# A mixture-of-experts kernel: the first expert's tokens gathered as high and low parts, and fewer zero products ahead of the router's last tile

## The reference

```
def moe_swiglu(h, w_router, w_gu, w_down):        # 8 experts, top 2
    t = h.reshape(-1, D)
    top_val, top_idx = lax.top_k(t @ w_router, TOP_K)
    top_w = jax.nn.softmax(top_val, axis=-1)
    gates = sum(one_hot(top_idx) * top_w)
    for e in range(N_EXPERTS):                     # silu(t@g) * (t@u) @ w_down[e], width 3584
        out = out + gates[:, e:e + 1] * swiglu(t, w_gu[e], w_down[e])
```

## Time and profile before

| | us |
|---|---|
| median of 3 runs | 1406.62 (1405.25 to 1407.14) |
| the profiled execution's own time | 1406.65 |
| its span in the trace | 1404.8 |
| TensorE busy | 1342.0 |
| VectorE busy | 1172.6 |
| ScalarE busy | 898.4 |

### The profile page before, as it was taken

The page is one execution under the profiler, slowest core; times in us unless marked ns, Lnnn a source line. Parts: engine busy times, 40 slices in busy tenths (PEclk is TensorE's granted clock), DMA queues, the critical chain, the costliest instruction groups (busy, mean ns, idle before and its releaser), DMA issues.

```text
span 1404.8 us, 19513 instructions
## 1 busy us (share of the span) xinstructions
PE 1342.0 (96%) x6901; PEld 1130.2 (80%) x6901; DVE 1172.6 (83%) x950; ACT 898.4 (64%) x745; POOL 76.4 (5%) x93
## 2 busy tenths in 40 slices
PE   5589999999999999999999999999999999999995
PEld 3489999789777888888888888888888888888883
DVE  5866777778869988889888888888888888888883
ACT  3143443464837777777777777777777777777771
POOL 2510000000120000000000000000000000000000
PEclk9779999999999999999999999999999999999998
DMA  9998888759168999999999999999999999999970
GB/s 363 383 326 276 313 309 313 282 196 385 46 233 293 410 393 360 383 383 390 359 392 388 357 395 373 383 367 385 387 350 400 383 362 387 373 391 360 411 285 32
DMA packets 210154, 476.18 MB, mean 339 GB/s; under 512 B 14928, under 2 KB 38560, under 8 KB 210096
## 3 DMA queue, kind: packets, MB, share of 16 engines
q1 hardware_dynamic: 205216, 459.07, 87.6%
q0 software_dynamic: 4880, 16.34, 3.8%
HBM read 466.43 MB, written 8.93 MB: 338 GB/s over the span
## 4 chain that ended last, share of the span: by engine, by line
PE 89%; DVE 7%; ACT 2%; issue 1%; DMA 1%; SPq 0%; DVEq 0%; POOL 0%; POOLq 0%; ACTq 0%
PE ps L1525 28%; PE ps L1527 27%; PE ps L1526 27%; PE ps L1918 2%; DVE rows L1099 1%; DVE rows L1094 1%; DVE wlo L1017 1%; PE ps L1543 1%; DMA raw<-w_mod 1%; DVE rows L1029 1%; DVE rows L1031 1%; PE ps L1750 0%; DVE wlo L1310 0%; PE ps L1884 0%; ACT whi L679 0%
## 5 line engine op out<-in xcount | busy, mean ns | idle before, releaser
L1310 DVE TENSOR_TENSOR wlx<-raw,whx 128x2048 fp32r<-128x2048 f32 x168 | 384.8, 2292 | 97.6 <-ACT whx L909 96.7
L1310 DVE TENSOR_TENSOR wlo<-raw,whi 128x2048 fp32r<-128x2048 f32 x168 | 384.2, 2288 | 4.4 <-ACT whi L909 3.0
L909 ACT ACTIVATE whi<-raw 128x2048 fp32r<-128x2048 f32 x168 | 322.2, 1919 | 88.6 <-PE ps L1527 87.4
L909 ACT ACTIVATE whx<-raw 128x2048 fp32r<-128x2048 f32 x168 | 322.2, 1919 | 82.9 <-PE ps L1527 82.9
L1525 PE MATMUL ps<-whi,thi 128*128 128x512 f32 x508 | 204.5, 402 | 1.0 <-DVE tlo L1282 0.6
L1527 PE MATMUL ps<-whi,tlo 128*128 128x512 f32 x508 | 198.5, 391 | 0.0
L1526 PE MATMUL ps<-wlo,thi 128*128 128x512 f32 x508 | 198.2, 390 | 0.0
L1525 PE MATMUL ps<-whx,thi 128*128 128x512 f32 x452 | 176.8, 391 | 0.5 <-DVE tlo L1282 0.5
L1527 PE MATMUL ps<-whx,tlo 128*128 128x512 f32 x452 | 176.1, 390 | 0.0
L1526 PE MATMUL ps<-wlx,thi 128*128 128x512 f32 x444 | 172.8, 389 | 0.0
L1525 PE MATMUL ps<-thi,whi 128*128 128x256 f32 x480 | 137.5, 286 | 3.1 <-DVE tlo L1021 3.1
(11 more groups left out here) (258 smaller groups left out, 1922.1 us busy)
## 6 DMA issues: line engine op xcount, KB each, us to landing
raw<-moe_w_gu SPq DMA_DIRECT2D x448, 512.0 KB, 6.1
raw<-moe_w_down SPq DMA_DIRECT2D x224, 512.0 KB, 6.3
raw<-w_mod SPq DMA_DIRECT2D x96, 512.0 KB, 5.3
raw<-ffn_w_gu SPq DMA_DIRECT2D x44, 512.0 KB, 5.1
raw<-w_qkv SPq DMA_DIRECT2D x24, 512.0 KB, 5.6
raw<-ffn_w_down SPq DMA_DIRECT2D x22, 512.0 KB, 4.4
raw<-w_o SPq DMA_DIRECT2D x8, 512.0 KB, 5.6
gain<-norm_g POOLq DMA_DIRECT2D x4, 512.0 KB, 4.9
```

The lines of the kernel that those rows point to most:

```text
L909: act.activation(m_hi[m % MRING], raw[:, r % RAW, :], ACT.Copy).then_inc(hi_ready, 1)
L1310: dve.tensor_tensor(m_lo[m % MRING], raw[:, r % RAW, :], m_hi[m % MRING].bitcast(F32), ALU.subtract).then_inc(unit_done, 1)
```

## The change

The gather of expert 0 is done on parts. The high and low parts of the token tiles are made as rows ahead of it: ScalarE writes `h_hi` (`token_high`, 128 x 1024 for each tile), VectorE `h_lo` (`token_low`). `sel_r` is the selection as fp32r. TensorE multiplies each part with `sel_r` by itself, high parts into banks 2 and 3, low parts into banks 4 and 1, so that `thi` and `tlo` are plain copies of the banks. ScalarE copies bank 3 of the router's second tile instead of VectorE. The 24 zero products become 8. In VectorE's stream the two copies of the low banks come ahead of the low part of unit 1, and `select(0)`, which the slot plan still needs in fp32, behind it.

More of the change, by code:

```diff
@@ L242, in build_trunk @@
         sb("scr_mid", [P, 2 * D])
-        sb("scr_end", [P, UNIT])
+        scr_end = sb("scr_end", [P, UNIT], F32R)
         wlx1 = sb("wlx1", [P, UNIT], F32R)
         wlx2 = sb("wlx2", [P, UNIT], F32R)
+        h_hi = scr_end[:, :].rearrange("p (t d) -> p t d", t=T)
+        h_lo = whx1[:, :].rearrange("p (t d) -> p t d", t=T)
+        sel_r = ahi[:, 0:T * P].rearrange("p (t s) -> p t s", t=T)
         o_hi = [whx1[:, :]] + [whi[:, (Q_WO + i) % SPL, :] for i in range(SPL)]
@@ L376, in build_trunk @@
         wo_ps = sem("wo_ps")
-        ht32_rest = sem("ht32_rest")
+        parts_hi = sem("parts_hi")
+        parts_lo = sem("parts_lo")
+        selr_ready = sem("selr_ready")
+        gl_ps = sem("gl_ps")
         counting_ready = sem("counting_ready")
@@ L1325, in _ @@
             expert_low(0, 0)
-            dve.wait_ge(ht_ps, 4 * 2 + 4)
-            dve.tensor_copy(ht32[:, 4:8, P:S], bank(3).rearrange("p (k s) -> p k s", k=4)).then_inc(ht32_rest, 1)
+            def token_low(t):
[3 more added lines that the diff above has]
+            token_low(0)
             dve.wait_ge(lg_ps, 1)
@@ L1837, in router @@
                     if k % 4 == 0:
[L1838 to L1841, removed]
+                        pe.wait_ge(ht32_ready, 2 * t + k // 4 + 1)
                     mm = pe.matmul(ps[:, 4, t * NE:t * NE + NE], ht32[:, k, t * P:t * P + P], wr[:, k, :],
@@ L1868, in experts @@
                 r0, j0, n0 = R_MOE + ps_no * NE * EXPERT_UNITS, ps_no * NE, ps_no * NE * NCE
-                def gather(j):
+                def gather():
+                    pe.wait_ge(selr_ready, T)
                     for b in range(2):
[L1873 to L1877, removed]
+                        for part, bk, done in ((h_hi, 2 + b, g_ps), (h_lo, LOW_BANK[b], gl_ps)):
[8 more added lines that the diff above has]
+                            mm.then_inc(done, 1)
                 def turn_gathered(e):
@@ L1968, in expert @@
                         down(c, n, m, e, first)
-                pe.wait_ge(sel_ready, T * j0 + T)
                 if ps_no == 0:
-                    gather(j0)
+                    gather()
                 else:
+                    pe.wait_ge(sel_ready, T * j0 + T)
                     pe.wait_ge(scat_done, 4 * ps_no)
```

## The result

| | kernel before | changed kernel |
|---|---|---|
| median us | 1405.97 (1404.34 to 1407.14, 5 runs) | 1412.83 (1411.14 to 1414.15, 5 runs) |
| ratio, 95% interval | | 1.0047 (1.0035 to 1.0058) |
| span of the profiled execution | 1404.8 | 1412.3 |

The changed kernel is 6.9 us slower; the interval is 4.9 to 8.2 us. Forecast were +5.9 and 1412.5. The ratio is worked out from all runs and is not exactly the quotient of the two medians (1.0049). The profiled execution of the changed kernel, 1414.15 us, is the longest of its five, so its trace shows 7.5 us of loss where the medians show 6.9.

A forecast was written before the change was run, and what follows sets the result against it. VectorE's order of work, not TensorE's gather, was taken to hold the first expert's start, and TensorE to pace the loop after it. 4.65 us late plus 1.2 for the clock gave +5.9, 1406.62 to 1412.5; range 1408.2 to 1416.8.

The forecast's parts named there:

- Step 1: Ahead of the router's second tile: 8 zero products instead of 24 bring the logits 0.5 us earlier, bounds -1.0 and +1.0.
- Step 2: Beside the router: VectorE swaps the bank-3 copy for `token_low(0)`, ScalarE takes more work; nothing on the path.
- Step 3: Expert 0's gather: 32 fp32r products take 6.0 us plus 0.2 to be seen, so it doesn't get shorter.
- rival (b): Gather: a narrow fp32r product costs two fp32 records, 8.8 + 0.2 us; +8.7 in all, 1415.3; chance 0.12.
- rival (a): Clock down through turn and router products, logits +1.0; gather all at 1.2 GHz, 0.8 more; +8.2, 1414.8; chance 0.17.
- (c): Gather: loads are cheap, products cost what zero products do, 3.4 + 0.2 us; 1409.9; chance 0.17.
- (d): Gather at 2.4 GHz and 0.053 us a product takes 1.9 us; +0.1, 1406.7, no change; chance 0.12.
- Step 4: VectorE at the first expert: low-bank copies put `expert_low(0, 1)` 6.45 us late and `times_up` 4.65 late.
- Step 5: First down products: TensorE idles 4.4 us ahead of them instead of 0.58, and the lower clock costs 1.2 us.

The follow-up runs named there:

- order_wide: order_before with 24 of the 32 gather products 256 columns wide, the extra columns written over; 1406.16 us, ratio 1.0002.
- order_before: Changed kernel with VectorE's order of the kernel before, nothing left out; 1408.75 us, ratio 1.0018.
- keep24: Changed kernel with 24 zero products ahead of the router's second tile, as before; 1412.53 us, ratio 1.0049.
- before_keep8: Kernel before with 8 zero products instead of 24 and nothing else; 1405.95 us, ratio 1.0000.
- slots64: Changed kernel with gather products 64 columns wide instead of 128, only 64 slots filled; 1412.97 us, ratio 1.0042.
- low_quarter: Changed kernel with three quarters of the gather's low products left out, 20 products instead of 32; 1409.64 us, ratio 1.0021.
- order_zeros20: order_before with 20 instead of 12 zero products between the router and the slot count; 1408.34 us, ratio 1.0019.
- after_again: Changed kernel run once more, nothing altered, as the measure for runs beside it; 1413.48 us, ratio 1.0044.
- warm_down: Changed kernel with 40 zero products in TensorE's wait ahead of the first down products; 1410.92 us, ratio 1.0035.
- order_wide_act: Changed kernel with VectorE's old order, wide gather products, `alo` ahead of unit 10's low part, 20 zeros before the slot count; 1404.07 us, ratio 0.9988.
- before_act_zeros: Kernel before with `alo` ahead of unit 10's low part and 20 instead of 12 zeros before the slot count, run twice; 1405.53 and 1405.33 us.

## Why the prediction was right

**What bounds the kernel.** Right. The delay by the first down products, 6.0 us, is found at the end whole, and where an experiment moved them by 2.6 us (order_wide against order_before, 453.21 and 455.82), its median moved by 2.6. VectorE's order was the limit: undoing it alone took 4.7 of 7.4 us; the rest was the gather at 1.2 GHz, which order_wide took away.

**Step 1, the zeros.** The turn did start as forecast, held by VectorE's tile. But I had the clock at 1.2 GHz until 417.8; in this execution it was up until 418.5, through the zeros and the eight turns (1.09 us), and fell in the router's products, where I had it up. The logits were forecast 0.5 us earlier; they came 0.24 later in the profiled execution (421.55) and 1.5 earlier in the second one (419.82), according to where the clock fell. The second lies beyond my bound of -1.0 by 0.5 us, the 0.45 by which the turn started ahead of my 417.0 there (416.55). So this term varies more than I allowed; what it is worth can't be told from nothing (keep24, before_keep8).

**Step 2.** Right: `token_low(0)` and the ScalarE work lie under waits that are longer.

**Step 3, the gather.** Mis-sized: 6.2 us with its result seen, measured 7.1. The price of a record, 0.213 us whatever its columns, was right (slots64), and rival (b), two records' price, is out. I let the clock come back half-way, as in the old gather. It didn't, in any of the seven traces of gathers of 128 columns or fewer that began at 1.2 GHz, low_quarter's shortened one among them. The upper bound of the step, 6.8 + 0.2, is what happened, and with it the second half of rival (a). With wide products it did come back inside the gather (order_wide). Rivals (c) and (d) asked for 3.4 and 1.9 us; even at 2.4 GHz it took 4.0 (order_zeros20), and at either level an fp32r record cost what an fp32 one does: no quicker load shows.

**Step 4, VectorE's order.** The sum has the right terms: `expert_low(0, 1)` is 8.05 us late instead of 6.45 (the gather's 0.9 and the logits' 0.7), and less what comes off, plus `select(0)`, less the slack, that makes 6.3; `times_up` was 6.0 late where 4.65 was forecast. What I said of TensorE beside it was wrong: it wasn't fed late by units 1 to 3. It ran from 431.85 to the end of unit 3, about 444.6 and not 443, without a wait; its first products were late and slow, and VectorE was later still.

How much of the 6.0 belongs to this one execution, the others show. Counted from the start of VectorE's low part of unit 0 (416.87 before, 416.70 in the changed kernel), the first down products come after 36.7 us before and 42.9 in the first trace, but after 41.5 to 41.8 in after_again, slots64, keep24 and warm_down, where the router's products ran at 2.4 GHz. There the delay is 4.8 to 5.2 us: near the 4.65, though partly by luck, since the gather was longer than forecast and the logits earlier.

**Step 5, the idle TensorE.** The loss was 1.5 us against 1.2 forecast, which is luck in part, for the length was wrong: 4.4 us of idling were forecast and 2.72 came, because I let TensorE finish unit 7 as soon as its low part was there. It has units 4 to 7 to do one after another from 445.1 on, when unit 4's low part is there, and the row of the wait puts their end at 456.85. With this wait the clock fell in four traces of five; in the fifth (low_quarter, 2.75 us) it stayed up. The way to the scatter shows what the fall costs, and warm_down that filling the wait saves it.

**Rival (a)** had the clock down through the turn and the router's products. It fell well within the router's products in two of the ten traces with eight zeros (the changed kernel's and before_keep8's) and in none of the four with 24; in the changed kernel's the eight turns themselves ran at 2.4 GHz. By the Trainium skill (TensorE: Matmul & The Clock Gate, Part 4: PE-mode transpose) transposes don't count as busy for the clock; these traces neither refute that nor need it. The medians show no worth of the zeros ahead of the turn that could be told from none.

The sum: 6.0 + 1.5 = 7.5 us is the profiled execution's loss, and its spans differ by 7.5. The medians differ by 6.9, and the forecast was 5.9. The gather was under-sized by 0.9 us in the profiled executions of the changed kernel (7.1 us in both), and the fall of the clock ahead of the down products cost 1.5 to 2.9 where 1.2 was put down; the logits' term varied by 1.7 us between two executions. How the missing 1.0 us of the medians divides among these wasn't measured.

## What to carry to other kernels

When an engine that works in strict order is the bound, the place of a wait in its stream counts for more than the length of the work that it waits for: two copies put ahead of the low parts cost 4.7 us; among them, in their old places, VectorE didn't wait for them at all. Splitting an fp32 product into two fp32r ones won nothing here, where each product has its own full weight load and few columns and costs the same at 64, 128 and 256 of them. And a wait of an otherwise busy TensorE can have a second price, the slower first products behind it, which filling the wait with zero products took away here.

## What the runs showed of the hardware

An fp32r product with its own 128x128 load costs 0.21 to 0.22 us at 1.2 GHz, whether it is 64, 128 or 256 columns wide (slots64, the changed kernel, order_wide), and 0.12 at 2.4 at 128 columns (order_zeros20) as at 256. The clock told them apart all the same. All six full gathers of 128 or 64 columns that began at 1.2 GHz stayed there for the whole 6.9 us. In the two wide ones (order_wide, order_wide_act) it was back 4.9 and 3.8 us after the gather's start, and in the four of fp32 products (the kernel before, before_keep8 and before_act_zeros twice) after 2.5 to 5.3 us. TensorE's busy share is 1.00 in the rows of either kind from the gather's second microsecond on, so that share didn't show which would get its clock back.

With a wait of 2.57 to 2.74 us ahead of the first down products the clock fell around their start in four traces, and with 2.75 us in a fifth it didn't; once fallen it cost between 1.5 and 2.9 us. One program thus has executions that differ by more than a microsecond from the clock: the changed kernel's five runs spread over 3.0 us, those of before over 2.8. One trace is one of these executions, and its starts are best compared from a point ahead of the change.
